# A decoder block on one NeuronCore: two more weight units in seven products, two attention heads one unit later, a pair of transposes one unit sooner

## What is computed

```python
h = rms_norm(x, norm_mix)
qkv..., gc, gates = split_cols(h @ w_in, IN_SPLITS)      # 3608 columns, and 3 x 2048 of gates
y_a = swa_attention(...)      # window of 128, 8 heads
y_b = stick_breaking(...)     # 4 heads of 128: log-sigmoids, a sum over later keys, exp, values
y_c = nsa_attention(...)      # compressed, selected and window branches, 8 heads
merged = sigmoid(g_a) * (y_a @ w_br_a) + sigmoid(g_b) * (y_b @ w_br_b) + sigmoid(g_c) * (y_c @ w_br_c)
x = x + merged @ w_out
h = rms_norm(x, norm_ffn)
x = x + (silu(h @ w_gate) * (h @ w_up)) @ w_down          # 5632 wide
out = rms_norm(x, norm_final)
```

## Time and profile before

| | us |
|---|---|
| median of three runs | 1344.67 |
| lowest and highest of the three | 1344.62, 1345.05 |
| the profiled execution, its own time | 1345.21 |
| its span, first to last instruction | 1343.5 |
| TensorE busy in the span | 1333.6 |
| VectorE busy | 1076.7 |
| ScalarE busy | 749.6 |
| GpSimd busy | 35.9 |
| moved by DMA | 261.20 MB, 194 GB/s on average |

### The profile page before, as it was taken

One profiled execution on the slowest core, in us unless ns is written; L12 is line 12 of the kernel. 1 busy time (PEld: TensorE's weight loads), 2 busy tenths in 40 slices (PEclk: granted clock), 3 DMA queues, 4 the chain that ended last, 5 costly groups with the idle time before them and its releaser, 6 DMA issues.

```text
span 1343.5 us, 27228 instructions
## 1 busy us (share of the span) xinstructions
PE 1333.6 (99%) x11555; PEld 1315.0 (98%) x11555; DVE 1076.7 (80%) x1507; ACT 749.6 (56%) x989; POOL 35.9 (3%) x62
## 2 busy tenths in 40 slices
PE   9999999999999999999999999999999999999997
PEld 8999999999999999999999999999999999999997
DVE  6554578888687898767899899889988889988984
ACT  7333457666556775465655655545544565555554
POOL 4000000000000000000000000000000000000003
PEclk9999999999999999999999999999999999999999
DMA  7777754455565567646566766655656576666553
GB/s 267 241 228 206 217 172 142 146 168 146 165 194 173 158 192 239 213 173 200 176 200 194 221 195 194 192 198 194 217 200 200 185 219 202 188 190 234 201 198 137
DMA packets 146458, 261.20 MB, mean 194 GB/s; under 512 B 11185, under 2 KB 28145, under 8 KB 146209
## 3 DMA queue, kind: packets, MB, share of 16 engines
q1 hardware_dynamic: 143824, 251.14, 59.1%
q0 software_dynamic: 2096, 7.57, 1.7%
q10 hardware_dynamic: 416, 0.75, 0.2%
HBM read 257.33 MB, written 2.10 MB: 193 GB/s over the span
## 4 chain that ended last, share of the span: by engine, by line
PE 92%; DVE 3%; ACT 2%; issue 1%; DMA 1%; SPq 0%; ACTq 0%; DVEq 0%
PE bank L794 14%; PE bank L795 14%; PE bank L796 14%; PE bank L846 13%; PE bank L848 13%; PE bank L849 13%; PE bank L813 3%; PE bank L815 3%; PE bank L816 3%; PE bank L782 2%; DVE weight_rings L1574 1%; ACT weight_rings L1272 1%; PE bank L1003 1%; PE bank L937 0%; DMA x<-in_x 0%
## 5 line engine op out<-in xcount | busy, mean ns | idle before, releaser
L1272 ACT ACTIVATE weight_rings<-raw_ring 128x1024 fp32r<-128x1024 f32 (+4 forms) x479 | 498.1, 1045 | 468.0 <-PE bank L796 147.8
L1574 DVE TENSOR_TENSOR weight_rings<-raw_ring,weight_rings 128x1024 fp32r<-128x1024 f32 (+4 forms) x479 | 576.8, 1208 | 191.7 <-ACT weight_rings L1272 187.1
L794 PE MATMUL bank<-weight_rings,h2T_hi 128*128 128x256 f32 x704 | 195.2, 277 | 0.0
L795 PE MATMUL bank<-weight_rings,h2T_hi 128*128 128x256 f32 x704 | 194.4, 276 | 0.0
L796 PE MATMUL bank<-weight_rings,h2T_lo 128*128 128x256 f32 x704 | 194.4, 276 | 0.0
L846 PE MATMUL bank<-weight_rings,hT_hi 128*128 128x256 f32 x550 | 155.7, 283 | 0.1
L849 PE MATMUL bank<-weight_rings,hT_lo 128*128 128x256 f32 x550 | 152.5, 277 | 0.0
L848 PE MATMUL bank<-weight_rings,hT_hi 128*128 128x256 f32 x550 | 152.5, 277 | 0.0
L794 PE MATMUL bank<-weight_rings,hT_hi 128*128 128x256 f32 (+3 forms) x476 | 139.2, 292 | 0.0
L795 PE MATMUL bank<-weight_rings,hT_hi 128*128 128x256 f32 (+3 forms) x476 | 137.4, 289 | 0.0
L796 PE MATMUL bank<-weight_rings,hT_lo 128*128 128x256 f32 (+3 forms) x476 | 137.3, 288 | 0.0
(11 more groups left out here) (372 smaller groups left out, 3483.1 us busy)
## 6 DMA issues: line engine op xcount, KB each, us to landing
raw_ring<-in_w_in SPq DMA_DIRECT2D x128, 512.0 KB, 3.6
raw_ring<-in_w_gate SPq DMA_DIRECT2D x88, 512.0 KB, 4.4
raw_ring<-in_w_up SPq DMA_DIRECT2D x88, 512.0 KB, 4.4
raw_ring<-in_w_down SPq DMA_DIRECT2D x88, 512.0 KB, 4.2
raw_ring<-in_w_out SPq DMA_DIRECT2D x32, 512.0 KB, 4.2
raw_ring<-in_w_in SPq DMA_DIRECT2D x40, 128.0 KB, 2.5
raw_ring<-in_w_br_c SPq DMA_DIRECT2D x16, 256.0 KB, 4.1
raw_ring<-in_w_br_a SPq DMA_DIRECT2D x16, 256.0 KB, 4.2
```

The lines of the kernel that those rows point to most:

```text
L794: pe.matmul(dst, x_hi, w_hi, start=opening, stop=False, skip_group_check=True)
L795: pe.matmul(dst, x_hi, w_lo, start=False, stop=False, skip_group_check=True)
L1272: act.activation(split_view(whi_flat, u), raw_view(u), ACT.Copy)\
L1574: dve.tensor_tensor(lo, w, hi.bitcast(F32), ALU.subtract).then_inc(lo_ready, 1)
```

## The change

Gate group 6 joins the groups whose units 3 and 5 are computed in seven products. The token sums for these two indices, made behind slots 56 and 59 before, are now made behind slots 49 and 51. The steps of heads 2 and 3 of stick-breaking come one slot later. The pair of transposes behind unit 9 now stands behind unit 8.

```diff
-GATES_BY_SEVENS = (7, 8, 9, 10, 11)
+GATES_BY_SEVENS = (6, 7, 8, 9, 10, 11)
...
-GATE_SUMS_SLOT = 56
+GATE_SUMS_SLOTS = (49, 51)
...
-GATE_SUM_AT.update({U_MIX + GATE_SUMS_SLOT + 3 * n: len(EARLY_SEVEN) + n for n in range(len(GATE_SEVEN))})
+GATE_SUM_AT.update({U_MIX + k: len(EARLY_SEVEN) + n for n, k in enumerate(GATE_SUMS_SLOTS)})
...
 def stick_slot(h, step):
-    return 76 + 6 * h + step
+    return 76 + 6 * h + (1 if h >= 2 else 0) + step
...
             def follow(u):
 
-                if u == UPC + 1:
+                if u == UPC:
                     pe.wait_ge(consts_ready, 1)
                     two_transposes(sc[:, 0, 0, :])
```

## The result

The changed kernel took **1348.18 us** (median of 9 runs, 1347.85 to 1350.49) beside 1345.05 for the kernel before (9 runs of the same session, 1344.62 to 1346.88): ratio 1.0027, 95% interval 1.0018 to 1.0036. It is slower by about 3 us; the forecast was 1344.15, and its range ended at 1345.4. The profiled execution took 1347.85 us with a span of 1346.1, against 1345.21 and 1343.5: 2.64 us more.

The account below looks back on a forecast made before the run. TensorE, busy for 99% of the span, was taken to bound the kernel. The terms -0.105 - 0.71 + 1.0 - 0.80 + 0.1 = -0.5 us, from the median 1344.67, gave 1344.15 us, range 1342.9 to 1345.4.

Parts of the forecast that it names:

- (a): Projection, unit 9: with the pair of transposes one unit sooner, matmuls take 113.3 in place of 117.7 ns, -0.105 us.
- (b): Gate group 6, slots 53 and 55: 21 matmuls each in place of 24, six at 117.7 ns, -0.71 us.
- (d): Heads 2 and 3 one unit later: slot 94's stall and slots 94 to 97's slow pace go, -0.80; slot 104 late, +0.1.
- (c): Gate group 6: 9.63 us of work added to VectorE's list makes slot 55 wait about 1.0 us.
- the walk's 354.1: Time at which VectorE's split for slot 54 would end, 0.5 us before TensorE comes at 354.6.
- the forecast stall at slot 55: TensorE waiting ahead of slot 55 for VectorE's low part of the hT sums: 1.0 us, bounds 0.5 to 1.3.
- VectorE in time: Rival, chance 0.17: the lateness at slot 55 does not arise, -1.5 us in all, 1343.15 us.
- the heads' shift gives nothing: Rival, chance 0.15: slot 94's stall moves to slot 104 or head 2's wait, slow pace returns, 1344.95 us.
- the slower rival: Chance 0.04: the moved pair does not set the pace, units 10 to 47 could stay at 117.7 ns, 1347.9 us.
- the 0.04 kept for what had not been thought of: Chance left for outcomes outside the forecast, with 0.60, and the three rivals; no size given.
- slower by over 0.2%: Whole kernel slower by more than 0.2% (2.7 us): chance 0.05, the slow-pace rival and half of the rest.

Follow-up runs that it names:

- experiment 8: The changed kernel with the pair of transposes behind unit 8 left out: 1352.41 us, one execution.
- experiment 2: The kernel before with only gate group 6 in seven products and its token sums behind slots 49 and 51: 1348.95 us, ratio 1.0031.
- experiment 9: The kernel before with only the steps of heads 2 and 3 one slot later: 1345.06 us, one execution.
- experiment 3: The changed kernel with 20 useless identity transposes on TensorE behind slot 53, ahead of its wait: 1346.91 us, ratio 1.0012.
- experiment 4: The changed kernel with VectorE reading softmax step 11's values behind slot 50's work, ahead of slot 55's weight sums: 1347.03 us, ratio 1.0010.
- experiment 5: The changed kernel with the second set of token sums behind slot 52 in place of 51: 1346.47 us, ratio 1.0011.
- experiment 6: The changed kernel with both sets of token sums made by GpSimd in place of VectorE: 1345.01 us, ratio 1.0000.
- experiment 7: The changed kernel with both token sums on GpSimd and step 11's values read one slot sooner by VectorE: 1344.62 us, ratio 0.9997.
- experiment 1: The changed kernel with gate group 6 back at eight products and its token sums at slots 56 and 59: 1344.92 us, ratio 0.9999.

## Why the prediction was wrong, by its steps

**(a)** held: the stream gained 0.11 us by unit 11 (0.105 forecast), and experiment 8 shows that the pair sets the pace. The sign it gave, unit 9 in 2.72 us, did not come: unit 9 takes 2.82 and unit 10 the 2.72, as the first spacing behind the pair is 0.20. **(b)** held: slot 53's 21 matmuls take 353.84 - 351.36 = 2.48 us against 2.83 for 24, and slot 55 gains 0.35. The rows' 117.7 ns was the right price. The 109 ns that the prediction cites beside it is, in that section of the Trainium skill (TensorE: Matmul & The Clock Gate, Back-to-back issue gap), the gap of an isolated matmul; the section says that in a stream the weight loads help to set the spacing. No run here has 109.

**(d)** held in its numbers: -0.79 us by slot 103 against -0.80, and +0.14 at slot 104 against +0.1, with slot 94 coming 1.39 us after its split where I had 1.4. Slot 104 waited for 0.02 us only; the rest is the stream's restart. Of the mechanism one half is shown, the stall of 0.39. That the slow pace of slots 94 to 97 (0.41) was left by that stall is not: in experiment 2 the stall stayed and the pace was fast. What sets it there stays open, so that half came out right partly by luck. In experiment 9, where no gate group 6 stands before it, the split ends 0.05 us ahead of the matmul too, and the gain is the same.

**(c)** failed, and it alone. Its price of VectorE's work was right: the low part of the hT sums, forecast to end at 359.3, ended at 358.93. Even the walk's 354.1 for slot 54's split was right (353.77). What failed is the sentence "On the way slot 54 needs its split", as the one thing that the walk asked of VectorE between slots 53 and 55. The reading of step 11's values also stood in that list, behind 8.07 of the 9.6 us (the 6.29 of slot 54's split and 1.78 for the second hT sums), and the text never asked who waits for it. Its waiter is not a unit but the transposes behind slot 53, by line 1012. They were 2.65 us late, the forecast stall at slot 55 never came (TensorE reached it at 362.43, 3.5 us after it was ready), and 1.0 us in the sum should have been 2.65. The evidence stood in the earlier trace rows: the reading at 348.83 was already the last thing ahead of the split for 55. The prediction's own prices give the stall: the reading comes at 348.83 - 1.00 + 8.07 - 0.105 = 355.80 (355.46 measured), takes 0.87, and the transposes follow 0.16 later, at 356.8, where TensorE would be ready at 354.46 - 0.105 - 0.353 = 354.0: 2.8 us.

The second error is of kind, not of size: every stall was priced at its own length. The granted clock of 1.00 in the kernel before (the page shows only 9, that is 90% or more, in each slice) was taken to stay, when it depended on TensorE not idling for so long, as experiment 3 shows. Behind 2.65 us of idleness the chip gave half the clock for some 3.4 us, and 1.5 us went there. With both put right the sum is -0.105 - 0.71 + 2.65 + 1.5 - 0.79 + 0.14 = +2.7. The stream became 2.83 us longer, the profiled execution 2.64 and the median 3.13; the 0.3 us by which the median goes beyond the stream are not explained.

No rival came true. *VectorE in time* was wrong in its premise (VectorE was busy for 5.86 of 6 us); *the heads' shift gives nothing* was refuted by the 0.75; the slower rival had the right size, 1347.9, for a reason that didn't arise. The outcome fell into the 0.04 kept for what had not been thought of, and, at 0.27%, into "slower by over 0.2%", which had 0.05. The range failed because its bounds of the stall, 0.5 to 1.3, came from the speed of VectorE's list and none from a forgotten waiter.

## What to carry to other kernels

When work is put into an engine's list, go through everything that stands behind the insertion and write down each one's waiter on the other engines, readings that free a buffer above all; checking only the units that the change is about misses them. Changing the order shifts the lateness to the next consumer (experiments 4 and 5), unless work leaves the list (6 and 7). An idle stretch of TensorE is not priced at its length alone: look at the granted clock behind it, and if the wait can't go, try splitting or filling it, which kept the clock here (experiments 5 and 3). Before reading a median, see whether the times lie in groups: experiment 4's did, and its median stands 1.6 us above what its trace shows.

## What was not expected of the hardware

- The clock fell to 0.50 behind one idle stretch of 2.65 us, in all three kernels that had it (the changed one, experiments 2 and 8), and not behind waits of 0.72, 1.15 and 1.44 us. Where between these it turns wasn't tried.
- Two inputs from SBUF cost VectorE a wait of 1 us beside GpSimd (1.67 for 0.68 us), and some 1.7 us over all its operations that ran beside GpSimd, so that moving 3.6 us of work to an idle engine gave VectorE only 1.8.
- In the profiled executions, kernels that are the same up to there reach unit 8 anywhere between 31.4 and 33.8 us, and a kernel's times fall into groups some 2 us apart (1344.5 to 1345.8 and 1346.5 to 1347.3 for the kernel before). The two seem to be one thing: the three profiled executions that reach unit 8 at 33.5 to 33.8 (experiments 1, 3 and 7) are also of the slower ones of their kernel, and the others reach it by 32.3. What sets this, and why slots 174 to 190 in experiment 1 and 19 to 21 in experiment 7 ran at the slow pace, stays open; it hides gains under 1 us from this timing.
